# Two chunks of the gather instead of four ahead of a tile's first gate products

## The chip, the cores and the metric

The kernel runs on one core of a Trainium2 chip. The metric is the device time of one execution in microseconds (us), the median of several runs. Before the change it is 2276.74 us, from three runs between 2275.95 and 2277.89 us.

## The reference, cut to what matters

All values are float32; there are 256 tokens of width 1024. The first block has two layers. Each ends in an expert layer with 16 experts, where every expert picks its 32 tokens by a router score:

```python
xe = h[bidx, idx]                               # the picked tokens' rows
a = jnp.einsum('becd,edf->becf', xe, w_gate)    # d = 1024, f = 1024
u = jnp.einsum('becd,edf->becf', xe, w_up)
ye = jnp.einsum('becf,efd->becd', jax.nn.silu(a) * u, w_down)
out = jnp.zeros_like(h).at[bidx, idx].add(gate[..., None] * ye)
```

The second block has one layer. It ends in a mixture of 32 experts (4 groups of 8, f = 512, two experts for each token), of which the kernel computes the same three products per expert. What comes ahead of the expert layers (attention, a scan, a long convolution, gates, the router) does not change here.

## The kernel before, in words

**Tiles.** Four experts with 32 slots each fill the 128 rows of TensorE, and such a group is called a tile. Each layer of the first block has 4 tiles (`tile_0` to `tile_3`). The second block has 8 (`tile2a` and `tile2b`, in a loop of 4 rounds); its loop over them is repeated if an expert has more tokens than 32 slots, which the router's count decides at run time.

**The gather.** Before an expert can multiply, the picked tokens have to be brought together. This is done by products with a 0/1 matrix. `gather(j)` (through `tile_slots`, L732 to L740) computes two of the 8 chunks of 128 channels (c = 2j and 2j+1) into one bank of PSUM: 4 matmuls, which the profile records as 8. ScalarE copies them to `x_slots` (L1488 by way of L1510 in the first block, L1515 in the second, where an offset is added). There are four gathers per tile, x0 to x3, and ScalarE copies them in this order. They use two banks in turn.

**The products.** Each tile reads its weights in units of 2 MiB: in the first block 24 units (8 gate, 8 up, 8 down; a gate unit holds one chunk c), in the second block 12 (4 gate, 4 up, 4 down; a gate unit holds two chunks). A unit is used by 8 matmuls (L768, or L792 for down), which are recorded as 16. Ahead of every even chunk of the gate TensorE waits for the copy x(c/2), which holds this chunk and the next one.

**Woven tiles.** With `woven` false (tiles 1 to 3 of each layer) all four gathers stand ahead of the products. With `woven` true (`tile_0` of both layers, and all 8 tiles of the second block) two gathers stand ahead, the third comes ahead of chunk 2 and the fourth ahead of chunk 4.

**Behind unit 0.** In `tile_0` of each layer TensorE runs `other_slots` (L1157 to L1169) right behind unit 0: some small products that make the picks of the later tiles.

**The weights' queue.** SyncE (SP) issues all loads of weights in one queue, in an order written out by hand. The first block has 10 places for units and the second 9. At the start of `tile_0` units 0 to 9 need no product of the tile; unit 10 goes where unit 0 was and waits until TensorE has done unit 0, unit 11 waits for unit 1, and unit 12 for unit 3. In the second block units 0 to 8 of the first tile are loaded ahead, and unit 9 waits for unit 0 (`free2`, L2898 to L2903). All of these loads go through L2778.

Of the kernel before, what the change touches and what calls it, by code (L numbers as in the profile page):

```python
# [350 lines left out]
def build(nc, io, tables):  # L351
# [4 lines left out]
    with ExitStack() as ctx:  # L356
# [316 lines left out]
        def _(pe):  # L673
# [14 lines left out]
            def to_act(reader):  # L688
                ring_a[0] += 1
                return take(ring_a[0] % 2, "act", reader)  # L690

            def to_dve(reader):
                ring_v[0] += 1
                return take(2 + ring_v[0] % 2, "dve", reader)
# [37 lines left out]
            def tile_slots(name, j, hn, pick_of):  # L732

                out = to_act(f"{name} x{j}")
                for c in (2 * j, 2 * j + 1):
                    cols = slice((c % 2) * P, (c % 2 + 1) * P)
                    for half in range(TH):
                        last = pe.matmul(out[:, cols], hn[:, half, c * P:(c + 1) * P], pick_of(half),
                                         start=half == 0, stop=half == TH - 1)
                last.then_inc(pe_done, pe_p.mark(f"{name} x{j}"))  # L740

            def expert_tile(name, prev, gather, loaded, spread_of, f_width, woven, place, behind=lambda u: None, back=None, turn=None):

                fc = f_width // P
                halves = f_width // 512
                per_unit = 2 // halves
                n_in = DC // per_unit

                between = (2, 4) if woven else ()
                for j in range(2 if woven else 4):  # L750
                    gather(j)
                if prev:
                    pe.wait_ge(act_done, act_at(f"{prev} y1", loops, **(back or {})))
                    pe.wait_ge(dve_done, dve_at(f"{prev} hid", loops, **(back or {})))
                for which, bank0 in (("gate", 4), ("up", 6)):
                    for n in range(n_in):
                        u = n + (n_in if which == "up" else 0)
                        loaded(u)
                        w = place(u).rearrange("p (e k f) -> p k e f", k=per_unit, e=TILE_E)
                        for k in range(per_unit):  # L760
                            c = n * per_unit + k
                            if which == "gate" and c % 2 == 0:
                                if c in between:
                                    gather(c // 2 + 1)
                                pe.wait_ge(act_done, act_at(f"{name} x{c // 2}", loops))
                            for f in range(halves):
                                for e in range(TILE_E):
                                    last = pe.matmul(banks[bank0 + f][32 * e:32 * e + 32, :],  # L768
                                                     x_slots[:, c, 32 * e:32 * e + 32],
                                                     w[:, k, e, f * 512:(f + 1) * 512],  # L770
                                                     start=c == 0, stop=c == DC - 1)
                        steps = [f"{name} unit {u}"] + ([f"{name} {which}"] if n == n_in - 1 else [])
                        last.then_inc(pe_done, pe_p.mark(*steps))
                        behind(u)

                if turn:
                    turn()
                pe.wait_ge(dve_done, dve_at(f"{name} hid", loops))
                for j in range(fc // 4):
                    out = to_act(f"{name} hidT{j}")  # L780
                    for f in range(4):
                        last = pe.transpose(out[:, f * P:(f + 1) * P], hid[:, (4 * j + f) * P:(4 * j + f + 1) * P],  # L782
                                            ident)
                    last.then_inc(pe_done, pe_p.mark(f"{name} hidT{j}"))
                pe.wait_ge(act_done, act_at(f"{name} hidT{fc // 4 - 1}", loops))
                for f in range(fc):
                    u = 2 * n_in + f
                    loaded(u)
                    w = place(u).rearrange("p (e d) -> p e d", e=TILE_E)
                    for d in range(2):  # L790
                        for e in range(TILE_E):
                            last = pe.matmul(banks[4 + d][32 * e:32 * e + 32, :], hidT[:, f, 32 * e:32 * e + 32],  # L792
                                             w[:, e, d * 512:(d + 1) * 512], start=f == 0, stop=f == fc - 1)
                    steps = [f"{name} unit {u}"] + ([f"{name} down"] if f == fc - 1 else [])
                    last.then_inc(pe_done, pe_p.mark(*steps))
                    behind(u)
                for j in range(4):
                    if j % 2 == 0:
                        pe.wait_ge(act_done, act_at(f"{name} y{j // 2}", loops))
                    out = to_dve(f"{name} add{j}")  # L800
                    for c in range(2):
                        last = pe.matmul(out[:, c * S:(c + 1) * S], y_sb[:, (2 * j + c) * P:(2 * j + c + 1) * P],  # L802
                                         spread_of(), start=True, stop=True)
                    last.then_inc(pe_done, pe_p.mark(f"{name} back{j}"))
# [110 lines left out]
            for layer in range(LAYERS):  # L915
# [256 lines left out]
                for t in range(TILES1):  # L1172
                    def loaded(u):
                        unit_ready(("tile", t, u), layer)

                    def place(u):
                        return slot(SLOT_OF[layer]["tile", t, u])

                    def behind(u):
                        if (t, u) == (0, 0):  # L1180
                            other_slots()
                        if (t, u) == (0, DC - 1):
                            pe.wait_ge(dve_done, dve_at("ada 5 cols", loops))
                        if (t, u) == (0, UNITS1_TILE - 1):
                            pe.wait_ge(dve_done, dve_at("spread", loops))
                        if layer == LAYERS - 1 and (t, u) in background:
                            background[t, u]()

                    def gather(j):
                        tile_slots(f"tile_{t}", j, hn_tok, lambda half: pick[:, half, t * P:(t + 1) * P])  # L1190

                    if t == 1:
                        pe.wait_ge(dve_done, dve_at("picked", loops))
                    expert_tile(f"tile_{t}", f"tile_{t - 1}" if t else None, gather, loaded, lambda: spread1[:, t, :], FE,
                                t == 0, place, behind)
# [237 lines left out]
            with pe.Fori(0, passes) as p:  # L1433
# [11 lines left out]
                with pe.Fori(0, TILES2 // 2) as t:  # L1445
                    loops["tile2"] = t
                    for h in range(2):
# [11 lines left out]
                        def turn():  # L1459
                            pe.wait_ge(dve_done, dve_at(f"{name} weighed", loops))  # L1460
                            out = to_act(f"{name} spread")
                            for half in range(TH):
                                last = pe.transpose(out[:, half * P:(half + 1) * P], weighed[:, half, :], ident)
                            last.then_inc(pe_done, pe_p.mark(f"{name} spread"))
# [1542 lines left out]
```

## Time and profile before

| | us |
|---|---|
| median of 3 runs | 2276.74 |
| profiled execution | 2275.23 |
| its span | 2273.4 |
| TensorE, matmuls busy | 1723.1 |
| VectorE busy | 660.5 |
| ScalarE busy | 554.9 |

In the rows of the profile PE is TensorE, PEld its weight loads, DVE VectorE, ACT ScalarE and SPq the queue of SyncE. A window row gives the length of the stretch, the busy time of each engine with its number of instructions, the granted TensorE clock (1.00 is 2.4 GHz, 0.50 is 1.2 GHz), the share of the 16 DMA engines that was busy, and the rate in GB/s. A timeline row gives start, length, engine, line, what is written and read, the count, and in brackets how long the engine was idle before and what ended that. The profiled execution lies 1.5 us below the median of the runs.

The core moves 748.74 MB in all, 329 GB/s over the span. Where it streams expert weights the rate is 409 to 410 GB/s.

### The profile page before, as it was taken

What the parts mean: (1) busy time and instruction counts of PE and PEld (TensorE: products, weight loads), DVE (VectorE), ACT (ScalarE), POOL (GpSimd) and SP (SyncE); (2) the same over time, 40 slices, a digit from 0 to 9 for tenths busy, and PEclk for the clock granted to TensorE, in tenths of its full rate; (3) what the DMA queues carried; (4) which work ended last, traced back from release to release, by engine and by line L of the source; (5) the groups of instructions that cost most, each with busy time, mean ns of one, the idle gap of its engine ahead of it and who ended that gap; (6) DMA issues with size and microseconds to landing.
All of it is one profiled execution on the core that took longest, in us unless ns stands there. A gap on an engine that the chain in (4) does not pass through costs nothing.

```text
span 2273.4 us, 29108 instructions
## 1 busy us (share of the span) xinstructions
PE 1723.1 (76%) x12754; PEld 1061.5 (47%) x12754; DVE 660.5 (29%) x1074; ACT 554.9 (24%) x849; POOL 0.2 (0%) x4
## 2 busy tenths in 40 slices
PE   7989976555555999996776767659999977666675
PEld 7978922120111897882222323238988622222222
DVE  3477510000000447650251111037557300000001
ACT  3356300000000436630110222033453301010101
POOL 0000000000000000000000000000000000000000
PEclk9999998887888999999788889889999987777776
DMA  9733899999999972489999999973425999999996
GB/s 366 261 121 104 305 407 409 409 409 409 409 409 408 353 254 99 144 311 407 410 406 403 403 406 406 409 290 112 148 93 185 391 409 410 410 410 410 410 409 251
DMA packets 226974, 748.74 MB, mean 329 GB/s; under 512 B 6064, under 2 KB 18608, under 8 KB 226224
## 3 DMA queue, kind: packets, MB, share of 16 engines
q1 hardware_dynamic: 226864, 747.11, 84.5%
q8 instruction: 89, 1.46, 0.3%
q14 instruction: 21, 0.17, 0.0%
HBM read 746.04 MB, written 1.05 MB: 329 GB/s over the span
## 4 chain that ended last, share of the span: by engine, by line
DMA 41%; PE 39%; SPq 13%; ACT 3%; DVE 3%; issue 2%; DVEq 0%; ACTq 0%
PE bank L711 19%; DMA ring<-w_expert_down 16%; SPq L2778 12%; DMA ring<-w_expert_up 11%; DMA ring<-w_expert_gate 6%; PE bank L714 5%; PE bank L768 3%; DMA arena<-moe_w_down 3%; PE bank L792 2%; DMA ring<-moe_w_up 2%; DMA ring<-ada_w 2%; PE bank L945 1%; DMA ring<-moe_w_down 1%; PE bank L802 1%; PE bank L965 1%
## 5 line engine op out<-in xcount | busy, mean ns | idle before, releaser
L768 PE MATMUL bank<-ring,arena 128*32 128x512 f32 x2560 | 384.9, 733 | 231.7 <-DMA ring<-w_expert_up 115.9
L792 PE MATMUL bank<-ring,arena 128*32 128x512 f32 x1280 | 213.7, 801 | 169.0 <-DMA ring<-w_expert_down 130.1
L711 PE MATMUL bank<-arena_parts,ring_parts 128*128 128x256 f32 x1376 | 313.8, 283 | 2.3 <-DVE ring_parts L2423 1.5
L768 PEld LDWEIGHTS bank<-ring,arena 128*32 128x32 f32 x2560 | 79.1, 123 | 497.3 <-DMA ring<-w_expert_up 167.0
L711 PEld LDWEIGHTS bank<-arena_parts,ring_parts 128*128 128x128 f32 x1376 | 233.2, 189 | 11.4 <-issue 3.0
L1488 ACT ACTIVATE arena<-bank 128x512 f32<-128x512 f32 (+1 forms) x150 | 76.1, 536 | 517.8 <-PE bank L782 259.0
L792 PEld LDWEIGHTS bank<-ring,arena 128*32 128x32 f32 x1280 | 40.5, 129 | 325.0 <-DMA ring<-w_expert_down 193.1
L2005 DVE TENSOR_TENSOR arena<-arena,bank 128x512 f32<-128x512 f32 x24 | 15.8, 685 | 580.7 <-PE bank L768 580.7
L711 PE MATMUL bank<-ring_parts 128*128 128x256 f32 x768 | 153.4, 289 | 13.3 <-DVE hnT_parts L2442 5.7
L711 PE MATMUL bank<-hnT_parts,ring_parts 128*128 128x256 f32 x544 | 154.7, 284 | 0.0
L711 PEld LDWEIGHTS bank<-ring_parts 128*128 128x128 f32 x768 | 125.5, 194 | 16.8 <-DVE hnT_parts L2442 6.9
L1532 ACT ACTIVATE arena<-bank 128x512 f32<-128x512 f32 x32 | 17.4, 594 | 378.8 <-PE bank L792 378.8
L711 PEld LDWEIGHTS bank<-hnT_parts,ring_parts 128*128 128x128 f32 x544 | 104.6, 192 | 0.2 <-issue 0.2
L2410 DVE TENSOR_TENSOR hT<-hT,bank 128x512 f32<-128x512 f32 x32 | 22.0, 688 | 274.1 <-PE bank L802 274.1
L711 PE MATMUL bank<-hnT_parts,arena_parts 128*128 128x256 f32 x352 | 99.3, 282 | 0.0
L711 PE MATMUL bank<-arena_parts 128*128 128x256 f32 x352 | 99.2, 282 | 0.0
L2157 DVE TENSOR_TENSOR ring_parts<-ring,arena_parts 128x2048 fp32r<-128x2048 f32 x30 | 68.7, 2291 | 83.1 <-ACT arena_parts L1591 83.1
L1790 ACT ACTIVATE ring_parts<-ring 128x2048 fp32r<-128x2048 f32 (+1 forms) x36 | 62.0, 1724 | 125.5 <-PE bank L711 101.0
L2634 DVE SCALAR_TENSOR_TENSOR hT<-bank,arena,hT 128x256 f32<-128x256 f32 x72 | 31.4, 479 | 200.7 <-PE bank L802 189.4
L802 PE MATMUL bank<-arena 128*128 128x256 f32 x256 | 79.7, 473 | 13.0 <-ACT arena L1532 11.3
L2423 DVE TENSOR_TENSOR ring_parts<-ring,ring_parts 128x2048 fp32r<-128x2048 f32 (+1 forms) x36 | 73.8, 2053 | 45.7 <-ACT ring_parts L1790 45.2
L802 PEld LDWEIGHTS bank<-arena 128*128 128x128 f32 x256 | 59.6, 242 | 49.7 <-issue 26.4
(351 smaller groups left out, 2385.5 us busy)
## 6 DMA issues: line engine op xcount, KB each, us to landing
ring<-w_expert_down SPq DMA_DIRECT2D x64, 2048.0 KB, 23.9
ring<-w_expert_up SPq DMA_DIRECT2D x60, 2048.0 KB, 23.6
ring<-w_expert_gate SPq DMA_DIRECT2D x56, 2048.0 KB, 23.6
ring<-w_in SPq DMA_DIRECT2D x34, 2048.0 KB, 10.8
ring<-moe_w_up SPq DMA_DIRECT2D x24, 2048.0 KB, 23.8
ring<-moe_w_gate SPq DMA_DIRECT2D x20, 2048.0 KB, 23.6
ring<-moe_w_down SPq DMA_DIRECT2D x16, 2048.0 KB, 23.8
arena<-moe_w_down SPq DMA_DIRECT2D x16, 2048.0 KB, 23.5
```

Source lines behind the costliest of these rows:

```text
L711: last = pe.matmul(out[:, n * S:(n + 1) * S], w[:, k, n * P:(n + 1) * P], x[:, k, :], start=first, stop=final)
L714: last = pe.matmul(out[:, n * JOB:(n + 1) * JOB], x[:, k, n * P:(n + 1) * P], w[:, k, :], start=first, stop=final)
L768: last = pe.matmul(banks[bank0 + f][32 * e:32 * e + 32, :], x_slots[:, c, 32 * e:32 * e + 32], w[:, k, e, f * 512:(f + 1) * 512], start=c ...
L792: last = pe.matmul(banks[4 + d][32 * e:32 * e + 32, :], hidT[:, f, 32 * e:32 * e + 32], w[:, e, d * 512:(d + 1) * 512], start=f == 0, stop ...
L802: last = pe.matmul(out[:, c * S:(c + 1) * S], y_sb[:, (2 * j + c) * P:(2 * j + c + 1) * P], spread_of(), start=True, stop=True)
L945: last = pe.matmul(out[:, 0:S], q[rows], k[rows], start=True, stop=True)
L1488: act.activation(out, in_, ACT.Copy, scale=scale).then_inc(act_done, act_p.mark(step))
L1790: act.activation(w_high2[i % 2][:, 0:JOBS2[i][3], :], job2_weights(i), ACT.Copy)\
L2157: dve.tensor_tensor(job_weights(JOBS[i], ring_parts), w, high_room(i).bitcast(F32), ALU.subtract)\
L2423: dve.tensor_tensor(job2_weights(i, ring_parts), job2_weights(i), w_high2[i % 2][:, 0:JOBS2[i][3], :].bitcast(F32), ALU.subtract).then_inc ...
L2634: last = dve.scalar_tensor_tensor(h3[:, n, :], bank[:, c, :], ada[:, gate * DC + n, 0:1], h3[:, n, :], ALU.mult, ALU.add)
L2778: sp.dma_start(dst, src).then_inc(loaded(at), 16)
```

## The change

In woven tiles only `gather(0)` stands ahead of the products. `gather(1)` comes ahead of the products of chunk 1. The third and the fourth gather stay where they were. What is computed does not change.

```diff
                 between = (2, 4) if woven else ()
-                for j in range(2 if woven else 4):
+                for j in range(1 if woven else 4):
                     gather(j)
...
                         for k in range(per_unit):
                             c = n * per_unit + k
+                            if which == "gate" and woven and c == 1:
+                                gather(1)
                             if which == "gate" and c % 2 == 0:
                                 if c in between:
                                     gather(c // 2 + 1)
                                 pe.wait_ge(act_done, act_at(f"{name} x{c // 2}", loops))
```

In `tile_0` of the layers chunk 1 is unit 1, so `gather(1)` then stands behind unit 0 and behind `other_slots`. In the second block chunks 0 and 1 are both in unit 0, so `gather(1)` then stands in the middle of that unit. The next gather follows ahead of chunk 2 in both.

## Rows read from the trace of the kernel before

**Rows 1.** The page, DMA and rate in 40 slices.
```profile
DMA  9733899999999972489999999973425999999996
GB/s 366 261 121 104 305 407 409 409 409 409 409 409 408 353 254 99 144 311 407 410 406 403 403 406 406 409 290 112 148 93 185 391 409 410 410 410 410 410 409 251
```
**Rows 2.** The page, chain that ended last, shares by engine.
```profile
DMA 41%; PE 39%; SPq 13%; ACT 3%; DVE 3%; issue 2%; DVEq 0%; ACTq 0%
```
**Rows 3.** Windows of the expert stages.
```profile
272.00:400.00 128.00, 90.36 (x754) 38.94 (x757) 15.49 (x47) 14.82 (x28) 0.00 (x0) 0.88 1.02 403
...
1006.00:1120.00 114.00, 76.05 (x620) 32.37 (x620) 16.35 (x53) 12.59 (x24) 0.00 (x0) 0.81 1.03 407
1120.00:1480.00 360.00, 254.11 (x1669) 110.11 (x1668) 74.12 (x86) 64.73 (x75) 0.00 (x0) 0.87 1.03 406
...
1804.00:1860.00 56.00, 44.77 (x338) 16.59 (x334) 4.56 (x11) 7.67 (x17) 0.00 (x0) 0.89 1.02 409
1860.00:1920.00 60.00, 41.13 (x242) 14.96 (x242) 4.67 (x11) 10.14 (x19) 0.00 (x0) 0.76 1.03 410
```
**Rows 4.** Timeline, start of the second block's first tile.
```profile
1794.96 3.78 PE L738 MATMUL bank<-arena 128*128 x16 [3.12 <-issue]
...
1797.07 0.63 ACT L1515 ACTIVATE arena<-bank,arena 128x128 f32<-128x128 f32 x2 [1.45 <-PE bank L738]
...
1798.67 2.42 PE L768 MATMUL bank<-arena 128*32 128x512 f32 x16
...
1801.02 1.16 PE L738 MATMUL bank<-arena 128*128 x8
1801.41 6.21 SPq L2778 DMA_DIRECT2D arena<-moe_w_down  x3
...
1802.10 1.92 PE L768 MATMUL bank<-arena 128*32 128x512 f32 x16
```
**Rows 5.** Windows of 2 us around the same place.
```profile
1798.00:1800.00 2.00, 2.00 (x12) 0.84 (x15) 1.06 (x5) 0.63 (x2) 0.00 (x0) 0.57 1.02 408
1800.00:1802.00 2.00, 2.00 (x20) 1.09 (x12) 0.00 (x0) 0.00 (x0) 0.00 (x0) 1.00 0.35 135
1802.00:1804.00 2.00, 2.00 (x19) 0.46 (x17) 0.00 (x0) 0.62 (x2) 0.00 (x0) 1.00 0.59 170
```
**Rows 6.** Timeline, start of `tile_0` of the second layer.
```profile
1018.00 3.65 PE L738 MATMUL bank<-arena 128*128 128x128 f32 x16 [0.83 <-issue]
1020.02 0.38 ACT L1488 ACTIVATE arena<-bank 128x256 f32<-128x256 f32 x1 [4.19 <-PE bank L738]
1021.58 1.93 PE L768 MATMUL bank<-arena 128*32 128x512 f32 x16
...
1023.57 5.11 SPq L2778 DMA_DIRECT2D arena<-w_expert_up  x2
...
1026.32 1.92 PE L768 MATMUL bank<-arena 128*32 128x512 f32 x16
```
**Rows 7.** Windows of 4 us, the second layer's `tile_0`.
```profile
1004.00:1008.00 4.00, 4.00 (x38) 4.00 (x37) 1.63 (x5) 2.94 (x4) 0.00 (x0) 0.98 0.68 180
...
1020.00:1024.00 4.00, 4.00 (x27) 2.21 (x27) 0.09 (x1) 0.77 (x2) 0.00 (x0) 0.81 1.03 412
```
**Rows 8.** Timeline, start of `tile_0` of the first layer.
```profile
285.46 2.02 PE L738 MATMUL bank<-arena 128*128 128x128 f32 x16 [0.83 <-issue]
286.63 0.38 ACT L1488 ACTIVATE arena<-bank 128x256 f32<-128x256 f32 x1 [2.36 <-PE bank L738]
287.42 1.92 PE L768 MATMUL bank<-arena 128*32 128x512 f32 x16
...
292.16 1.93 PE L768 MATMUL bank<-arena 128*32 128x512 f32 x16
```
**Rows 9.** Timeline, TensorE in a later tile of the loop.
```profile
1896.80 1.92 PE L768 MATMUL bank<-arena 128*32 128x512 f32 x16 [1.78 <-ACT arena L1515]
...
1908.36 3.12 PE L768 MATMUL bank<-ring,arena 128*32 128x512 f32 x16 [2.03 <-DMA ring<-moe_w_up]
```

## The prediction

> **What bounds the kernel now.** I read the slices first. The DMA row stands at 9 in three long stretches at 403 to 410 GB/s, with valleys between them, where the attention, the scan and the router run [rows 1]. The stretches are the expert stages. The chain of waits agrees: DMA makes up 41% of it, the SP queue 13% and TensorE 39% [rows 2]. Then I read the windows of the stages that hold woven tiles. From 272 us, from 1006 us and from 1804 us on the DMA share is 1.02 to 1.03, while TensorE has 76 of 114 us or 41 of 60 us of matmuls [rows 3]. In an expert stage time is therefore bytes over rate. TensorE counts only where it lets the DMA run dry. So the question for this change is not whether the first products start earlier, but when units are *finished*, because that opens a place for the next load, and whether the DMA is idle at that moment. There are three kinds of places: `tile_0` of two layers, the first tile of the second block, and the seven further tiles of its loop.
>
> **The second block's first tile, the place that counts.** Before, both gathers start at 1794.96 and unit 0 at 1798.67, and unit 0 is finished at 1801.09 [rows 4]. SP issues the next load at 1801.41, 0.3 us later. The DMA has by then run out of work: it moves 135 GB/s in 1800 to 1802 and 170 in 1802 to 1804 [rows 5]. At 410 GB/s the 0.34 MB of the latter window are 0.8 us, so bytes flow again at about 1803.2, 1.8 us after the issue. From there on the stage is at 409 to 410 GB/s to its end. Every 0.1 us by which unit 0 is finished later is 0.1 us on the end of the kernel.
>
> Unit 0 holds chunks 0 and 1 here. Both versions therefore run the same 32 records (16 of gathers, 16 of products) before unit 0 is finished; the change cannot shorten this work. What it takes away is the cover of one wait. The copy x0 begins at 1797.07 and ends at 1797.70 [rows 4]; it hangs on the first gather alone, whose 8 records end at 1794.96 + 3.78/2 = 1796.85. Today TensorE spends that time on the second gather, which ends after the copy. In the changed kernel it stands idle from 1796.85 to about 1797.8 (the copy's end and 0.1 us for the signal): 0.95 us.
>
> This is mostly time at half clock, so its cost is less than its length. The granted clock is 0.57 in 1798 to 1800 and 1.00 after [rows 5]: a rise from 1.2 to 2.4 GHz at 1800 - 0.14 x 2 = 1799.72. I count the work in full-clock time. Before: 4.76 us at half clock make 2.38, and 1.37 us at full clock (1799.72 to 1801.09), in all 3.75. Cutting gather and product into smaller groups costs a little too. At full clock a pair of gathers takes 1.96 us start to start (285.46 to 287.42) [rows 8], and a single one 1.08 (1801.02 to 1802.10) [rows 4]; two singles are 0.20 more than a pair. That makes 3.95. After: until 1799.72 there are 4.76 - 0.95 = 3.81 us of work at half clock, 1.91; the other 2.04 run at full clock, and unit 0 is finished at 1801.76. **The sum is +0.67 us**, if the clock rises at the same instant. The bounds: nothing, if the wait overlaps more of the gather's tail than I think (a gain is excluded, because the same work stands ahead of the mark); at the other end all of it at half clock, 1794.96 + 0.95 + 2 x 3.95 = 1803.81, +2.7 us.
>
> After that units 1, 2 and on are later by the same 0.7 us, and so are the loads that wait for them. Unit 10 waits for unit 1, finished 2.9 us after unit 0 (1804.02); one load takes 5.1 us (2.10 MB at 0.41 MB per us). It is issued while the load of unit 9 still runs, before and after.
>
> **`tile_0` of the two layers.** Here chunk 1 is a unit of its own. Unit 0 needs only the first gather and comes *earlier*: x0 is there at 287.01 and at 1020.40, and unit 0 starts at 287.42 and 1021.58 [rows 6, 8]. With 0.1 us for the signal the gain on unit 0 is 0.3 us in the first layer and 1.1 us in the second. It frees the place for unit 10. But at this moment the DMA is busy with units 8 and 9 (share 1.03, 412 GB/s in 1020 to 1024) [rows 7], so I price the earlier issue at nothing; its bound is the whole 1.4 us.
>
> Unit 1 comes later. TensorE now has a gap between the end of the first gather and the copy's end: in the first layer 0.6 us (286.5 to 287.1), in the second 0.7 (1019.8 to 1020.5). There unit 1 is finished at 1028.24 [rows 6], and with half of the gap (half clock) and 0.1 for the cut about 0.5 us later in the new order. Is the DMA dry by then? Units 6 to 10 are 10.5 MB, of which 0.72 MB had come by 1008 (180 GB/s x 4 us) [rows 7]; the rest at 407 GB/s lasts until 1032.0. Unit 11 is issued at about 1028.5 and needs 1.8 us to its first bytes, 1030.3. That leaves 1.7 us of cover, and 0.5 is used. In the first layer unit 1 is finished at 294.09 [rows 8]; five units at 403 GB/s from 272 on last until 298, so the cover is 1.8 us against 0.7. Both price at nothing. The work that hides them is the backlog of loads; without it each would cost 0.5 to 0.7 us. `other_slots` comes earlier together with unit 0, and what is left behind it (`gather(1)`, unit 1, `gather(2)`, unit 2) waits for no copy, since x1 now has the whole of unit 1 to arrive.
>
> **The seven further tiles.** In one of them TensorE is idle for 1.78 us before unit 0 already, for a copy that is late on ScalarE's side, and 10 us later it waits 2.03 us for a load [rows 9]. The windows there show a DMA share of 1.03 and 410 GB/s [rows 3]. The new order adds at most about 1 us ahead of unit 0 and TensorE then waits that much less for the next load: nothing.
>
> On ScalarE nothing is queued between x0 and x1 but the copies themselves, and what follows x3 is as late as before or by 0.7 us. SP's order does not change, and no DMA is moved.
>
> **Total.** +0.7 us on the profiled execution: 2275.23 becomes 2275.9. On the median of the runs, which lies 1.5 us above it, 2276.74 becomes 2277.4. A difference below 0.2% (4.6 us) is what a measurement of this kernel can't tell from none.
>
> **A rule weighed.** Before unit 0 the trace shows TensorE idle for 3.12 us, then dense work from 1794.96 on, and the clock up at 1799.72 [rows 4, 5]; in the second layer dense work starts at 1018.00, and the clock of 0.81 in 1020 to 1024 puts the rise at 1021.5 [rows 6, 7]. The Trainium skill ("TensorE: Matmul & The Clock Gate", section "What's actually happening") says that the half clock is the default, and that sustained activity releases it. By that rule a gap of 0.95 us in the middle of the climb may put the rise off; by my sum it does not. The two waits of 4.8 and 3.5 us differ, so the rows don't settle it. What it would cost is the first rival.
>
> **Rivals.**
> 1. *The clock rises later.* If the rise moves by the gap, to 1800.67, the work until then is 2.38 again and unit 0 ends at 1800.67 + 1.57 = 1802.24: +1.15 us, 2277.9. If it doesn't come before unit 0 is finished, +2.7 us, 2279.4. For it: the gap falls into the climb. Against: the two rises seen came after different lengths of work.
> 2. *The layers give the time back.* If the DMA's backlog were shorter than I count, unit 10's earlier issue would count: up to -1.4 us, against +0.7: 2276.0. For it: the earlier issue is real. Against: share 1.02 to 1.03 all through.
> 3. *The second layer's stream runs dry (the other side).* If the gap keeps the clock at 1.2 GHz through unit 1 of the second layer, the 8.5 us of full-clock work from 1018.00 to 1028.24 (1.75 until 1021.5, 6.74 after) take 17.0, and with the gap unit 1 ends at 1035.7, 7.4 us late. Less the 1.7 us of cover, 5.7 us are lost, +0.7 from the second block: 2283.1, slower by 0.28%. It decides once unit 1 is over 1.7 us late, and passes 0.2% when it is over 5.6 us late. Against: nothing in the rows shows a rise that late after dense work.
> 4. *The loop's tiles are not covered.* Seven times 0.95 us and 0.7: +7.4, 2284.1. For it: it is where most of the edited instructions run. Against: the waits for loads in every such tile.
>
> **Chances.** The forecast (0 to +1.1 us) 0.60; the first rival 0.16; the second, with a change that simply isn't seen, 0.16; the third 0.03; the fourth 0.02; 0.03 for something that I don't see. The likeliest is 2277.4. The range takes in the bounds -0.7 (2276.0) and +2.7 (2279.4) and 1.1 us on either side, for the runs spread over 1.9 us: 2274.9 to 2280.5. Only rivals 3 and 4 leave it on the slow side. Faster 0.02, same 0.93, slower 0.05.
>
> **What the changed profile would show.** In the second block's first tile an idle time of 0.9 to 1.0 us ahead of the first L768 rows, released by ACT L1515; those at about 1797.8 on the old time axis; the SP issue at about +0.7; the valley in the rate as much longer. In the layers, unit 10 issued 0.3 and 1.1 us earlier, unit 11 some 0.5 us later, and no dip below 1.0 in the share between 1028 and 1036. In the loop fewer microseconds of waits for `ring<-moe_w_up`, and the same 410 GB/s. The prediction is wrong if the SP issue comes earlier in the second block, if a dip appears in the layers or the loop, or if the time differs by more than 3 us.

## The result, and the profile after

The changed kernel takes 2282.21 us, the median of 18 runs (2275.16 to 2285.64), against 2277.61 us for the kernel before (18 runs, 2273.84 to 2281.92). The ratio is 1.0016, with a 95% interval from 1.0009 to 1.0024, so 2.0 to 5.5 us slower. (The two medians alone stand 4.6 us apart, a ratio of 1.0020.) The second time it was measured it gave 1.0025 (1.0013 to 1.0037). I had forecast +0.7 us, with a range that ended at 2280.5.

The two profiled executions lie 8.0 us apart (spans 2273.4 and 2281.5), and most of this is not the change. SP's issue times cut both into the same pieces. "Last load ahead" is the last issue of the second block that does not wait for `tile2a`'s products.

| piece of the span | before | after |
|---|---|---|
| start to the issue of unit 7, layer 0 (no woven tile yet) | 271.8 | 274.4 |
| unit 8 to the first load of `tile_1`, layer 0 | 67.1 | 66.9 |
| the same, layer 1 | 78.7 | 78.2 |
| last load ahead to the issue of unit 9, second block | 17.72 | 20.21 |
| from there to the last load | 425.9 | 425.9 |
| last load to the first store | 41.2 | 38.9 |

The first row is already 2.6 us apart, ahead of any changed instruction. Such steps also stand in the head of layer 1 and in the tail, in both directions. The clock is low for different times in them (6.8 us before and 10.2 us after in the first row); whether that makes all of a step was not tested. One pair of profiles can't weigh a change of 4 us here. The pieces in which the changed code stands can be compared, and one of them differs: the second block's first tile, +2.5 us, of which 0.4 lie ahead of the first gather's start (11.28 us after the last load ahead in the old kernel, 11.67 in the new one) and 2.1 behind it. Its timeline, with the columns of [rows 4]:

```profile
1803.23 2.07 PE L738 MATMUL bank<-arena 128*128 x8 [3.09 <-issue]
...
1805.33 0.62 ACT L1517 ACTIVATE arena<-bank,arena 128x128 f32<-128x128 f32 x2 [1.42 <-PE bank L738]
...
1806.39 1.94 PE L770 MATMUL bank<-arena 128*32 128x512 f32 x8 [1.10 <-DVE arena L2724]
...
1808.26 2.08 PE L738 MATMUL bank<-arena 128*128 x8
...
1810.27 1.18 PE L770 MATMUL bank<-arena 128*32 128x512 f32 x8
...
1811.38 1.16 PE L738 MATMUL bank<-arena 128*128 x8
1811.77 6.21 SPq L2780 DMA_DIRECT2D arena<-moe_w_down  x3
```

The gap is there, 1.10 us. (Its releaser is printed as VectorE; the wait in the code is for the copy x0 of L1517, which ended at 1805.95. The products begin 0.44 us after that, where I had put 0.1 for the signal.) But what follows is slow as well. The first four products take 1.94 us and the second gather 2.08; in [rows 4] a gather takes 1.08 once the clock is up. SP's issue comes 8.54 us after the first gather's start, where it came at 6.45. The windows of 2 us answer [rows 5]:

```profile
1806.00:1808.00 2.00, 1.61 (x8) 0.21 (x8) 1.13 (x7) 0.00 (x0) 0.00 (x0) 0.50 1.03 412
1808.00:1810.00 2.00, 2.00 (x12) 1.74 (x8) 0.14 (x1) 0.00 (x0) 0.00 (x0) 0.50 0.20 78
1810.00:1812.00 2.00, 2.00 (x15) 0.87 (x15) 0.00 (x0) 0.62 (x2) 0.00 (x0) 0.86 0.03 8
1812.00:1814.00 2.00, 2.00 (x21) 0.76 (x20) 0.00 (x0) 0.62 (x2) 0.00 (x0) 1.00 0.58 129
```

The clock is at 0.50 up to 1810 and at 0.86 in the next window, so it rises at 1810.6: 7.3 us after the first gather's start instead of 4.8. The DMA's valley is deeper and longer too (78, 8 and 129 GB/s). Behind it the stream is as before, also in the loop's seven further tiles; this row answers the last one of [rows 3]:

```profile
1860.00:1920.00 60.00, 38.49 (x246) 13.74 (x246) 4.66 (x11) 10.25 (x19) 0.00 (x0) 0.84 1.03 409
```

In the layers this one execution shows no loss. Layer 1, to be set beside [rows 6]: the clock is up, unit 0 starts 1.70 us after the gather, and its place is free (1026.99) 3.7 us after the gather's start instead of 5.6.

```profile
1023.32 1.13 PE L738 MATMUL bank<-arena 128*128 128x128 f32 x8 [0.83 <-issue]
1024.49 0.38 ACT L1490 ACTIVATE arena<-bank 128x256 f32<-128x256 f32 x1 [2.35 <-PE bank L738]
1025.02 1.92 PE L770 MATMUL bank<-arena 128*32 128x512 f32 x16 [0.56 <-ACT arena L1490]
...
1026.99 6.20 SPq L2780 DMA_DIRECT2D arena<-w_expert_up  x2
```

### The profile page after: what moved, and what is told of

Same layout as the page of the kernel before. It is cut to its first block, busy times and chain, and to the rows that moved or that the text cites. A ratio compares the mean times of both kernels' runs of the same rounds, so it can differ in the third digit from the quotient of the medians.

```text
span 2281.5 us, 29110 instructions
## 1 busy us (share of the span) xinstructions
PE 1725.7 (76%) x12754; PEld 1060.9 (47%) x12754; DVE 660.5 (29%) x1074; ACT 555.6 (24%) x849; POOL 0.2 (0%) x4
## 4 chain that ended last, share of the span: by engine, by line
PE 40%; DMA 39%; SPq 12%; ACT 4%; DVE 3%; issue 2%; DVEq 0%; ACTq 0%
PE bank L711 19%; DMA ring<-w_expert_down 17%; SPq L2780 12%; DMA ring<-w_expert_up 11%; DMA ring<-w_expert_gate 6%; PE bank L714 4%; PE bank L770 4%; DMA arena<-moe_w_up 3%; PE bank L794 2%; PE bank L804 1%; PE bank L738 1%; PE bank L947 1%; DMA ring<-moe_w_down 1%; DMA ring<-moe_w_up 1%; PE bank L967 1%
## 5 line engine op out<-in xcount | busy, mean ns | idle before, releaser
L770 PE MATMUL bank<-arena 128*32 128x512 f32 x512 | 72.1, 684 | 30.3 <-DMA arena<-moe_w_up 20.1
L804 PE MATMUL bank<-arena 128*128 128x256 f32 x256 | 73.4, 441 | 13.7 <-ACT arena L1534 11.3
L1593 ACT ACTIVATE arena_parts<-ring 128x2048 fp32r<-128x2048 f32 x30 | 57.4, 1916 | 102.3 <-PE bank L711 70.7
```

Source lines behind the costliest of these rows:

```text
L770: last = pe.matmul(banks[bank0 + f][32 * e:32 * e + 32, :], x_slots[:, c, 32 * e:32 * e + 32], w[:, k, e, f * 512:(f + 1) * 512], start=c ...
L1593: act.activation(high_room(i), job_weights(JOBS[i]), ACT.Copy)\
```

## The experiments

Each kernel was timed with 11 or 12 runs against 29 to 35 of the kernel before on the same chip, and profiled once; the row "after" is the first measurement, 18 against 18. "+x us" within a tile counts from the start of its first gather. The piece of the second block is the one of the table above.

| kernel | ratio (95% interval) | second block's piece, us | issue at | clock low until |
|---|---|---|---|---|
| before | 1 | 17.72 | +6.45 | +4.8 |
| after | 1.0016 (1.0009 to 1.0024) | 20.21 | +8.54 | +7.3 |
| rep_after | 1.0025 (1.0013 to 1.0037) | 20.20 | +8.49 | +7.2 |
| only_layers | 1.0012 (1.0001 to 1.0023) | 17.71 | +6.28 | +4.4 |
| only_second | 1.0011 (1.0001 to 1.0022) | 20.21 | +8.63 | +7.5 |
| gap_alone | 1.0018 (1.0006 to 1.0029) | 21.78 | +8.85 | +9.2 |
| fill_all | 0.9990 (0.9981 to 0.9999) | 18.63 | +7.23 | +4.5 |
| fill_again | 1.0004 (0.9993 to 1.0015) | 18.63 | +6.93 | +3.9 |
| fill_layers | 0.9995 (0.9985 to 1.0004) | 17.69 | +5.98 | +3.8 |
| late_second | 1.0011 (1.0001 to 1.0021) | 18.60 | +7.11 | +7.7 |
| warm_before | 1.0004 (0.9995 to 1.0013) | 17.08 | +4.26 | none |
| warm3_before | 0.9993 (0.9983 to 1.0003) | 18.28 | +5.44 | +2.6 |
| fill_warm3 | 0.9995 (0.9983 to 1.0007) | 19.74 | +6.59 | +2.0 |

The piece repeats closely: 17.69 to 17.72 us in the three profiles whose second block is as before (before, only_layers, fill_layers), 20.20 to 20.21 in the three with the new order, 18.63 in both with the filled gap.

**rep_after: the changed kernel again.** No edit.

> The changed kernel once more. Theory A (clock): the new order delays the end of unit 0 in the second block's first tile by 2 us or more, because TensorE stays at 1.2 GHz through all of unit 0; from the first gather's start to SP's next issue it then takes about 8.5 us again (before: 6.45) and the time is 2 to 3 us above before. Theory B (chance): the clock rose late in that one execution only; here the stretch takes 7.1 us and the time is 0.7 us above before. Theory C (layers): the time is 3 us or more above before with the stretch at 7.1 us, and a dip in the rate stands in tile_0 of a layer.

Measured: 20.20 us and +8.49, the same as the first time. Theory B (chance in one execution) has fallen. But the ratio of 1.0025 is 5.7 us, more than the second block's 2.5.

**only_layers and only_second: the two halves of the change.**

```diff
-                for j in range(2 if woven else 4):
+                split = woven and halves == 2        # only_layers; only_second: halves == 1
+                for j in range(1 if split else 2 if woven else 4):
                     gather(j)
...
+                            if which == "gate" and split and c == 1:
+                                gather(1)
```

> The new order in tile_0 of the two layers alone; the second block as before. Theory A and theory B: within 0.5 us of before (ratio 1.000). Theory C: 1.5 us or more above before, with unit 11 issued after the loads of units 8 to 10 have ended.

> The new order in the 8 tiles of the second block alone. Theory A: 2 to 3 us above before, the stretch from the first gather's start to SP's next issue 8.5 us, and from there to the last load the same distance as before (416 us). Theory B: +0.7 us, stretch 7.1 us. Theory C: +0.7 us or less. If instead the loop's later tiles cost something, the distance from that issue to the last issue grows.

Measured: 1.0012 and 1.0011, 2.7 and 2.5 us, each with an interval that only just stays above nothing (0.2 to 5 us). So both halves cost, neither theory A nor theory C holds alone, and their sum agrees with the whole (1.0016 and 1.0025) within the noise. For the second block the time is that of its piece. The layers I had priced at nothing. In the profile of only_layers both of them begin with a low clock; layer 0 of it:

```profile
285.25 2.01 PE L738 MATMUL bank<-arena 128*128 128x128 f32 x8 [0.83 <-issue]
287.82 3.64 PE L771 MATMUL bank<-arena 128*32 128x512 f32 x16 [0.56 <-ACT arena L1491]
...
294.56 1.22 PE L738 MATMUL bank<-arena 128*128 128x128 f32 x8
295.71 3.50 PE L771 MATMUL bank<-arena 128*32 128x512 f32 x16
```

Unit 0 takes 3.64 us and unit 1 3.50, where [rows 6] has 1.93 and 1.92. This is not one long low stretch but two. The clock comes up at 292.1, between the units, and falls again from 295.5 to 298.9, over unit 1:

```profile
288.00:290.00 2.00, 2.00 (x12) 0.47 (x11) 0.00 (x0) 0.00 (x0) 0.00 (x0) 0.50 1.03 414
...
292.00:294.00 2.00, 2.00 (x15) 1.71 (x14) 1.18 (x3) 0.00 (x0) 0.00 (x0) 0.97 1.02 408
...
296.00:298.00 2.00, 2.00 (x12) 0.40 (x8) 0.26 (x1) 0.20 (x1) 0.00 (x0) 0.50 1.00 397
```

Unit 1 ends at 299.2 and unit 11 is issued 14.0 us after the gather's start. By then the loads have run out:

```profile
296.00:300.00 4.00, 4.00 (x23) 1.25 (x16) 0.26 (x1) 0.20 (x1) 0.00 (x0) 0.63 0.79 315
300.00:304.00 4.00, 4.00 (x36) 1.25 (x35) 0.00 (x0) 0.38 (x1) 0.00 (x0) 1.00 0.86 304
304.00:308.00 4.00, 4.00 (x40) 1.78 (x43) 0.00 (x0) 1.67 (x2) 0.00 (x0) 1.00 0.99 357
308.00:312.00 4.00, 4.00 (x44) 1.22 (x40) 0.00 (x0) 0.00 (x0) 0.00 (x0) 1.00 1.00 366
```

The kernel before has 407 to 411 GB/s in these four windows. The difference is 1.19 MB, or 2.9 us at 410 GB/s. Whether a layer loses anything depends on whether the clock happens to be low when its gather starts. The piece from unit 8 to the first load of `tile_1`, over all profiles with the old order or the new one without filling:

| `tile_0`, order | clock at the gather | low until | unit 11 issued | piece, us (layer 0 / layer 1) |
|---|---|---|---|---|
| old | up (6 times of 10) | | +8.7 to +10.1 | 67.0 to 68.4 / 78.0 to 79.1 |
| old | low (4 times) | +3.1 to +3.7 | +10.2 to +10.3 | 67.9 / 78.6 to 79.1 |
| new | up (3 times of 6) | | +9.5 to +11.1 | 66.9, 67.5 / 78.2 |
| new | low (3 times) | +6.5 to +6.9 | +13.9 to +14.0 | 70.8 / 81.8, 81.8 |

About three us are lost in the last row and nothing in the others. In all three tiles of that row the clock also fell again over unit 1 (from +9.9 or +10.3 on), and in none of the four of the second row. From unit 10's issue to unit 11's 4.7 us pass in the second row, and 7.6 to 7.8 in the last; 1.1 us of the difference is `gather(1)`, which now stands between the two (new order, clock up: 5.8 us in two tiles), and most of the rest is unit 1 at low clock. Such a second stretch alone does no harm: layer 0 of the changed kernel's first profile has one (+6.9 to +10.3, unit 11 at +11.1) behind a unit 0 in time, and loses nothing. Rep_after's layer 1 shows the dry stream too, with 218 GB/s in the window in which the loads had run out:

```profile
1034.00:1038.00 4.00, 4.00 (x40) 1.77 (x36) 0.00 (x0) 0.38 (x1) 0.00 (x0) 1.00 0.67 218
```

With half of the tiles hit that makes about 3 us for two layers; measured are 2.7.

**fill_all and fill_layers: the gap filled.** Now theory G says that the gap keeps the clock low, theory O that the order does (narrow products earlier). The filling is two products that nobody reads, in all woven tiles or only in the layers:

```diff
                     gather(j)
+                if woven:                            # fill_layers: if split
+                    for _ in range(2):
+                        pe.matmul(banks[0][:, 0:P], hn_tok[:, 0, 0:P], ident, start=True, stop=True)
```

> The new order everywhere, and in the gap between the first gather and the wait for x0 two products (128x128 by 128x128, four records) that nobody reads, about 0.95 us at half clock. Theory G (the gap keeps the clock low): in the second block the rise comes 4.4 to 4.8 us after the first gather's start again instead of 7.2 to 7.5, SP's issue at +7.0 instead of +8.5; in tile_0 of the layers a low stretch that begins with the gather lasts 3.4 us and not 6.8, and unit 11 is issued by +10.5; the time is 0.5 to 1.5 us above before instead of 4 to 5. Theory O (not the gap but the order: narrow 128x32 products where gathers of 128x128 stood): the rise stays at +7.3, SP's issue comes at +8.6 or later, and the time stays 4 us or more above before.

> The new order with the filled gap in tile_0 of the layers alone, the second block as before. Theory G: no stream runs dry in the layers (from the issue of unit 8 to the loads' end 67 to 68 us in the first and 78.2 to 79.2 us in the second layer, not 70.8 and 81.8) and the time is within 0.7 us of before. Theory O: as with the new order and no filling, 2 to 3 us above before.

Measured: ratios of 0.9990 and 0.9995, so the loss is gone. The clock is low until +4.5 in the second block, and in a layer whose gather starts at low clock until +3.4 and +3.0 (layer 1 of both), not +6.5 to +6.9. The pieces there are 78.67 and 78.72 us, the clock does not fall again over unit 1, and unit 11 is issued at +10.9 and +10.7. Fill_all, second block:

```profile
1800.86 2.07 PE L738 MATMUL bank<-arena 128*128 x8 [3.08 <-issue]
1802.72 1.06 PE L754 MATMUL bank<-cst,arena 128*128 128x128 f32 x4
...
1804.00 1.70 PE L773 MATMUL bank<-arena 128*32 128x512 f32 x8 [0.22 <-DVE arena L2727]
...
1805.62 1.16 PE L738 MATMUL bank<-arena 128*128 x8
...
1806.71 1.06 PE L773 MATMUL bank<-arena 128*32 128x512 f32 x8
...
1808.09 3.30 SPq L2783 DMA_DIRECT2D arena<-moe_w_down  x2
```

The filling (L754) stands in the gap. The second gather takes 1.09 us to the next start (1805.62 to 1806.71) where it took 2.01 (1808.26 to 1810.27), and the issue comes at +7.23. The order is that of the changed kernel, so theory O has fallen. One window of each kernel, 4 to 8 us after its first gather's start, shows the clock side by side (before, after, fill_all):

```profile
1798.96:1802.96 4.00, 4.00 (x32) 1.57 (x28) 0.49 (x2) 1.07 (x4) 0.00 (x0) 0.90 0.53 189
```
```profile
1807.23:1811.23 4.00, 4.00 (x24) 1.99 (x16) 0.49 (x2) 0.62 (x2) 0.00 (x0) 0.58 0.29 116
```
```profile
1804.86:1808.86 4.00, 4.00 (x36) 2.16 (x32) 0.49 (x2) 0.62 (x2) 0.00 (x0) 0.94 0.42 165
```

A rival is that the low stretch merely began at another moment. It doesn't hold: in fill_layers (old order in the second block) and in rep_after (new order) the stretch began at the same -3.0 us, and it ended at +3.8 and at +7.2. The windows from 4 to 8 us after the first gather's start, fill_layers first:

```profile
1802.70:1806.70 4.00, 4.00 (x37) 1.63 (x32) 0.50 (x2) 1.07 (x4) 0.00 (x0) 1.00 0.56 185
```
```profile
1805.60:1809.60 4.00, 4.00 (x24) 1.99 (x16) 0.49 (x2) 0.63 (x2) 0.00 (x0) 0.59 0.31 125
```

**gap_alone: the gap without the new order.**

```diff
                 for j in range(2 if woven else 4):
                     gather(j)
+                    if woven and j == 0:
+                        pe.wait_ge(act_done, act_at(f"{name} x0", loops))
```

> The old order, with one wait added in all woven tiles: TensorE waits for the copy x0 between the first and the second gather. Nothing is reordered, only the gap is there. Theory G (the gap keeps the clock low): the second block's low stretch ends at +7.2 to 7.5 us instead of 4.4 to 4.8 and the issue comes at about +8.5; in a layer whose low stretch begins with the first gather it lasts 6.8 us; the time is 3 to 5 us above before, as with the changed kernel. Theory O (the order): the rise stays at +4.6, the issue comes at +6.9, and the time is 0.5 us above before.

Measured: 1.0018, and the clock low until +9.2, even later than expected. The low stretch had begun earlier here (-11.2 us, against -2.1 to -3.0 in the profiles before and after), and the first gather came 12.9 us after the last load ahead instead of 11.3. So not all of the 4.1 us by which the second block's piece is longer belong to the gap. In the second block both gathers and the whole of unit 0 run at half clock:

```profile
1800.62 2.07 PE L738 MATMUL bank<-arena 128*128 x8 [3.09 <-issue]
...
1803.52 2.07 PE L738 MATMUL bank<-arena 128*128 x8 [0.83 <-ACT arena L1517]
1805.52 3.64 PE L770 MATMUL bank<-arena 128*32 128x512 f32 x16
...
1809.09 1.51 PE L738 MATMUL bank<-arena 128*128 x8
1809.47 0.39 SPq L2780 DMA_DIRECT2D arena<-moe_w_down  x1
```

Layer 1 is the clean case: its low stretch begins with the gather (-0.3), as in rep_after, and lasts until +6.5, not +3.1 to +3.7 as in the old order without the gap. The clock falls again over unit 1, and the piece is 81.6 us. So the gap alone, without the new order, brings the late rise and a loss of the same size: 1.0018 (1.0006 to 1.0029) against 1.0016 and 1.0025.

**late_second: a gather less ahead of unit 0's end.** The layers as before; in the second block `gather(1)` at `c == 2`.

> Layers as before; in the second block one gather ahead and the second one only behind unit 0, so that unit 0 has a gather less ahead of its end. Theory G: the gap keeps the clock at 1.2 GHz through unit 0, issue at 1.9 + 1.1 + 3.3 + 0.3 = +6.6 us, as much as before (6.45), time within 0.5 us of before. Theory O: no worse. If the clock rose at +4.5 the issue would be at +5.6 and the time 0.9 us below before.

Measured: 1.0011 (0.2 to 4.8 us), where I had expected 0.5 us at most, a piece that is 0.9 us longer, and the issue at +7.11, not +6.6. The clock stays low until +7.7, past unit 0; the gap costs more than the missing gather saves.

```profile
1797.51 2.07 PE L738 MATMUL bank<-arena 128*128 x8 [3.09 <-issue]
1800.67 3.64 PE L771 MATMUL bank<-arena 128*32 128x512 f32 x16 [1.10 <-DVE arena L2725]
```

**warm_before, warm3_before, fill_warm3: work in the 3.1 us ahead of the first gather.** Six or three idle products behind "rank", in the old order or with the filled gap:

```diff
             last.then_inc(pe_done, pe_p.mark("rank"))
+            for _ in range(6):                       # the other two: 3
+                pe.matmul(banks[0][:, 0:S], ones, cst[:, C_IOTA:C_IOTA + S], start=True, stop=True)
```

> The old order, and six products whose result nobody reads (128x128 by 128x256, into bank 0) in the 3.1 us in which TensorE waits for the first picks of the second block. Theory A: the clock doesn't fall to 1.2 GHz there, so both gathers and unit 0 run at 2.4 GHz: from the first gather's start to SP's issue 4.1 us instead of 6.45, the DMA's valley shrinks to about nothing, and the time is 1.5 to 2.4 us below before. If the clock were not what sets this stretch it stays at 6.4 us and the time is that of before or up to 1 us above it.

> The old order with three idle products instead of six ahead of the first gather of the second block. Six delayed the gather by 1.5 us, since they ran at half clock for 4.5 us where 3.1 were free. Three take 2.6 us at half clock and delay nothing. If they keep the clock up or lift it in time: from the last load ahead of the gap to the next issue 15.6 us instead of 17.7 (with six 17.1), and 2 us below before. If three are too little work for the clock: 17.7 and no change.

> The filled gap and the three idle products ahead of the second block's first gather. If the products lift the clock before the gather: from the last load ahead to the next issue 15.8 us (before 17.7, filled gap alone 18.6) and 2 us below before. With the single execution of the three products at hand (18.3 us, the clock low until +2.6) more likely 18 us and no change from before.

Measured: with six the issue came at +4.26, as expected, and yet the time is 1.0004. The clock fell 0.3 us after the products had begun and stayed low until 0.7 us ahead of the gather. They took 4.5 us of the 3.1 that were free and pushed the gather back:

```profile
1796.47 4.52 PE L1430 MATMUL bank<-cst 128*128 128x256 f32 x12
1800.83 1.95 PE L738 MATMUL bank<-arena 128*128 x16
1802.87 1.92 PE L768 MATMUL bank<-arena 128*32 128x512 f32 x16
```

So the piece shrank by 0.6 us only. With three the clock stayed low until +2.6 and +2.0, and the pieces are 18.28 and 19.74 us. In both, as in gap_alone, the clock had been low since 11 us or more ahead of the gather, and the gather came 12.8 and 13.1 us after the last load ahead instead of 11.3; one profile each can't part this from what the products do. Both miss my better case; their times can't be told from before.

**fill_again.** The kernel of fill_all.

> The new order with the filled gap once more, for its time: 0.9990 of before with an interval from 0.9981 to 0.9999 was more than theory G gives, which has no gain over before (+0.8 us in the second block, unit 0 earlier in the layers at no value). So 0.9995 to 1.0005 is expected; below 0.9985 again would mean that something is gained that I have not found.

Measured: 1.0004, as expected. The 0.9990 of fill_all is not repeated, and it was the only interval of the study that lay below 1. No version that beats the kernel before has been found.

## Why the prediction was wrong

- **What counts is when units are finished, and where the DMA is dry: right.** The loop's seven tiles cost nothing. From the second block's first waiting issue to the last load all profiles have 425.1 to 426.1 us, before and after alike.
- **The second block's work and gap: right in size.** 0.95 us of gap were forecast, 1.10 measured; the term that was short is the 0.1 us from the copy's end to the products, 0.44 in the trace. With the clock rising as before the piece grew by 0.9 us (18.63 against 17.72, fill_all), where the sum had +0.67.
- **The step that failed: "The sum is +0.67 us, if the clock rises at the same instant."** It doesn't. I had seen that the gap falls into the climb, and made the later rise a rival of 0.16. In all three profiles of the new order the clock came up at +7.2 to +7.5 instead of +3.8 to +4.8, and the piece grew by 2.5 us. My bound for a rise after unit 0 was +2.7, so its price was about right and its chance was not. The Trainium skill ("TensorE: Matmul & The Clock Gate", "What's actually happening") states that sustained activity releases the half clock, which spoke for the rival. Layer 1 of gap_alone (low until +6.5) and of fill_all (+3.4) agree with it.
- **"Both price at nothing" for the layers failed too, by the mechanism of rival 3.** I took [rows 6] with the rise at 1021.5 and left it there. With the gap the low stretch lasts about 3.3 us longer and covers unit 0, the clock falls again over unit 1, unit 11 is issued 3.6 us later (+13.9 instead of +10.3), and about 3 us are lost. By my cover of 1.7 us such a delay would have lost 1.9. In only_layers the two windows of the valley lose 2.0, and the two behind it another 0.9 (357 and 366 GB/s): I had let the stream come back at full rate. I had given the rival 0.03 and priced it, for the second layer alone, as one low stretch from the gather through unit 1, at 5.7 us; in only_layers the first layer lost as much as the second.
- **Unit 0 of the layers comes earlier: right**, 0.3 us (+3.67 against +3.94) at high clock, and of no value. At low clock it comes later (+6.3 against +5.4 to +5.6).
- **The range** had the second block's bound in it and nothing for the layers. Together they are some 5 us, and the median fell 1.7 us outside. Of this 0.9 us is the base: the sum stood on 2276.74 from three runs, and 18 runs give 2277.61.

What stays open: why about half of the layers' tiles start at low clock, why the clock falls a second time over unit 1 where the first rise was late, and why the same kernel's runs spread over 10 us. I can only say that single low stretches of the clock fall in different places from one execution to the next.

## What to carry to other kernels

A wait that looks free, because the same work stands before and after it, still is a gap in TensorE's activity. Where it falls into a climb of the clock, price the later rise first and the idle time second. When moving work out of a wait's cover, leave something in its place: here two idle products took back what the new order had cost (0.9990 and 1.0004 against 1.0016 and 1.0025), though not more.

Before judging a change of a few us by two profiles, cut both at the same DMA issues and compare only the pieces that hold the changed code.

## What the runs showed of the hardware

A gap of 1.1 us (second block) or 0.6 us (layers) between two pieces of work at low clock put the rise to 2.4 GHz off by about 3 us, in all six places of the new order where the clock was low at the first gather. Filled with four records of matmul it did not, in four of four (fill_all and fill_again in the second block, layer 1 of fill_all and fill_layers). Where the rise was late in a layer, the clock fell again some 10 us after the gather's start, over unit 1, in four of four tiles, layer 1 of gap_alone among them. Of the six tiles with low clock at the gather and a rise at +3.0 to +3.7, none had such a second fall.

A stream of 2 MiB loads that ran dry was not back at once: with the next issue at +14.0 us it moved 315, 304, 357 and 366 GB/s in four windows of 4 us, where 407 to 411 are usual. The clock also decides what idle products are worth: six of them took 4.5 us, mostly at 1.2 GHz (0.68 and 0.50 in the windows from 1796 to 1800), where 3.1 us were free.
